# A gated recurrence and a long convolution, run among the weight blocks that follow them

## The reference, cut to what matters

```python
def hgrn2_chunked(q, k, v, log_f):
    B, S, H, DK = q.shape
    DV = v.shape[-1]
    nc = S // HG_CHUNK
    def to_chunks(t):
        return t.astype(jnp.float32).reshape(B, nc, HG_CHUNK, H, t.shape[-1]).transpose(0, 3, 1, 2, 4)
    q, k, v, log_f = to_chunks(q), to_chunks(k), to_chunks(v), to_chunks(log_f)
    b = jnp.cumsum(log_f, axis=3)
    b_last = b[:, :, :, -1:, :]
    q_t = q * jnp.exp(b)
    k_t = k * jnp.exp(-b)
    causal = jnp.tril(jnp.ones((HG_CHUNK, HG_CHUNK), dtype=bool))
    scores = jnp.einsum('bhntd,bhnsd->bhnts', q_t, k_t)
    scores = jnp.where(causal, scores, 0.0)
    o_intra = jnp.einsum('bhnts,bhnsv->bhntv', scores, v)
    k_end = k * jnp.exp(b_last - b)
    d_state = jnp.einsum('bhnsd,bhnsv->bhndv', k_end, v)
    decay = jnp.exp(b_last[:, :, :, 0, :])
    def step(state, inp):
        dec, ds = inp
        return dec[..., None] * state + ds, state
    s0 = jnp.zeros((B, H, DK, DV), jnp.float32)
    _, s_start = lax.scan(step, s0, (jnp.moveaxis(decay, 2, 0), jnp.moveaxis(d_state, 2, 0)))
    s_start = jnp.moveaxis(s_start, 0, 2)
    o_inter = jnp.einsum('bhntd,bhndv->bhntv', q_t, s_start)
    o = o_intra + o_inter
    return o.transpose(0, 2, 3, 1, 4).reshape(B, S, H, DV)
...
def hybrid_ab_mixer(x, w_in, lb, hg_norm_g, cv_w, cv_b, cv_ln_g, cv_ln_b, w_out):
    B, S, _ = x.shape
    h = x @ w_in
    q, f_pre, i_v, g, a, a_gate = jnp.split(
        h, [HG_WIDTH, 2 * HG_WIDTH, 3 * HG_WIDTH, 4 * HG_WIDTH, 4 * HG_WIDTH + CV_CH], axis=-1)
    lb = lb.astype(jnp.float32)
    f_pre = f_pre.astype(jnp.float32)
    f = lb + (1.0 - lb) * jax.nn.sigmoid(f_pre)
    k = (1.0 - lb) * jax.nn.sigmoid(-f_pre)
    log_f = jnp.log(f)
    heads = lambda t: t.reshape(B, S, HG_HEADS, -1)
    o = hgrn2_chunked(heads(q), heads(k), heads(i_v), heads(log_f))
    o = o * lax.rsqrt(jnp.mean(jnp.square(o), axis=-1, keepdims=True) + RMS_EPS)
    o = o.reshape(B, S, HG_HEADS * HG_DV) * hg_norm_g.astype(jnp.float32) * jax.nn.silu(g.astype(jnp.float32))
    u = a * jax.nn.sigmoid(a_gate)
    u = lax.conv_general_dilated(
        u, cv_w.astype(u.dtype), window_strides=(1,), padding=[(CV_K - 1, 0)],
        dimension_numbers=('NWC', 'WIO', 'NWC'), feature_group_count=CV_CH) + cv_b
    u = jax.nn.silu(layer_norm(u, cv_ln_g, cv_ln_b))
    y = jnp.concatenate([o.astype(x.dtype), u.astype(x.dtype)], axis=-1)
    return y @ w_out
...
```

## Time and profile before

| | |
|---|---|
| median of 3 runs | 1424.27 us (1422.57 to 1424.51) |
| the profiled execution | 1421.73 us, its span 1419.9 us |
| mean granted TensorE clock | 0.967 |
| TensorE busy | 1333.7 us (94% of the span) |
| VectorE busy | 857.3 us (60%) |
| ScalarE busy | 658.9 us (46%) |
| chain that ended last | PE 82%, DVE 9%, ACT 3%, DMA 3%, issue 2% |
| one weight load | 1024 KB, 5.0 to 5.3 us from issue to landing |

### The profile page before, as it was taken

One profiled execution on the slowest core, in us unless ns is written; L12 is line 12 of the kernel. 1 busy time (PEld: TensorE's weight loads), 2 busy tenths in 40 slices (PEclk: granted clock), 3 DMA queues, 4 the chain that ended last, 5 costly groups with the idle time before them and its releaser, 6 DMA issues.

```text
span 1419.9 us, 23502 instructions
## 1 busy us (share of the span) xinstructions
PE 1333.7 (94%) x9429; PEld 1248.6 (88%) x9429; DVE 857.3 (60%) x1164; ACT 658.9 (46%) x995; POOL 61.6 (4%) x72
## 2 busy tenths in 40 slices
PE   4999998999999998989997889899999999799996
PEld 4999997889998987889986788899999898799995
DVE  5566576775764544568796554655555755655555
ACT  4445676444447666345642344343433353334341
POOL 0011011000110000000000000100000000000000
PEclk9999999999989999989998899899999999899998
DMA  6555533345543332545550353655555444355552
GB/s 205 179 178 181 175 120 119 121 153 180 180 140 120 119 99 80 211 152 178 178 178 0 119 178 108 226 180 193 191 177 186 140 149 138 130 188 194 181 179 86
DMA packets 167747, 219.68 MB, mean 155 GB/s; under 512 B 3643, under 2 KB 151302, under 8 KB 167670
## 3 DMA queue, kind: packets, MB, share of 16 engines
q1 hardware_dynamic: 164422, 206.67, 44.5%
q0 software_dynamic: 3040, 11.20, 2.6%
q10 hardware_dynamic: 208, 0.74, 0.1%
HBM read 217.54 MB, written 1.05 MB: 154 GB/s over the span
## 4 chain that ended last, share of the span: by engine, by line
PE 82%; DVE 9%; ACT 3%; DMA 3%; issue 2%; POOL 0%; DVEq 0%; SPq 0%; ACTq 0%
PE bank L488 23%; PE bank L489 23%; PE bank L490 23%; DVE w_lo L1535 2%; PE bank L736 1%; DVE small L1559 1%; DVE h L1676 1%; ACT w_hi L1048 1%; DMA w_raw<-in_e_w_mem_kv 1%; PE bank L696 1%; PE bank L715 1%; PE bank L923 1%; DVE att L1597 1%; PE bank L748 1%; DMA w_raw<-in_o_w_out 1%
## 5 line engine op out<-in xcount | busy, mean ns | idle before, releaser
L1535 DVE TENSOR_TENSOR w_lo<-w_raw,w_hi 128x1024 fp32r<-128x1024 f32 x388 | 471.7, 1223 | 394.6 <-ACT w_hi L1048 391.3
L1048 ACT ACTIVATE w_hi<-w_raw 128x1024 fp32r<-128x1024 f32 x388 | 408.5, 1056 | 467.3 <-PE bank L490 368.9
L488 PE MATMUL bank<-u_hi,w_hi 128*128 128x256 f32 x1088 | 314.5, 289 | 3.3 <-DVE u_lo L1657 3.3
L489 PE MATMUL bank<-u_lo,w_hi 128*128 128x256 f32 x1088 | 311.5, 286 | 0.0
L490 PE MATMUL bank<-u_hi,w_lo 128*128 128x256 f32 x1088 | 311.3, 286 | 0.0
L488 PE MATMUL bank<-w_hi,y_hi 128*128 128x512 f32 (+1 forms) x656 | 234.6, 358 | 10.2 <-issue 7.5
L488 PE MATMUL bank<-w_hi,u_hi 128*128 128x256 f32 x832 | 238.3, 286 | 0.0
L489 PE MATMUL bank<-w_lo,u_hi 128*128 128x256 f32 x832 | 236.5, 284 | 0.0
L490 PE MATMUL bank<-w_hi,u_lo 128*128 128x256 f32 x832 | 236.5, 284 | 0.0
L489 PE MATMUL bank<-w_lo,y_hi 128*128 128x512 f32 (+1 forms) x656 | 231.1, 352 | 0.0
L490 PE MATMUL bank<-w_hi,y_lo 128*128 128x512 f32 (+1 forms) x656 | 230.6, 352 | 0.0
(11 more groups left out here) (273 smaller groups left out, 1318.6 us busy)
## 6 DMA issues: line engine op xcount, KB each, us to landing
w_raw<-in_e_w_in SPq DMA_DIRECT2D x28, 1024.0 KB, 5.0
w_raw<-in_o_w_in SPq DMA_DIRECT2D x28, 1024.0 KB, 5.2
w_raw<-in_ffn_wg SPq DMA_DIRECT2D x22, 1024.0 KB, 5.3
w_raw<-in_ffn_wu SPq DMA_DIRECT2D x22, 1024.0 KB, 5.3
w_raw<-in_ffn_wd SPq DMA_DIRECT2D x22, 1024.0 KB, 5.0
w_raw<-in_ab_w_in SPq DMA_DIRECT2D x12, 1024.0 KB, 5.2
w_raw<-in_e_w_out SPq DMA_DIRECT2D x8, 1024.0 KB, 5.0
w_raw<-in_o_w_out SPq DMA_DIRECT2D x8, 1024.0 KB, 5.2
```

Of the source, the lines that this page charges most:

```text
L488: pe.matmul(out_ap, ah, bh, start=start, stop=False, skip_group_check=True)
L489: pe.matmul(out_ap, ah, bl, start=False, stop=False, skip_group_check=True)
L1048: act.activation(w_hi[:, at:at + 1024], w_raw[:, at:at + 1024], ACT.Copy).then_inc(hi_done, 1)
L1535: v.tensor_tensor(w_lo[:, at:at + 1024], w_raw[:, at:at + 1024], w_hi[:, at:at + 1024].bitcast(F32), ALU.subtract).then_inc(lo_done, 1)
```

## The change

The mixer's small products go between the units of `ab_nat`, `xk0` and `xv0`, and between the halves of such a unit: the turn of the keys into the second `ab_nat` unit, one state product per half unit from the third on, the taps behind units, the outputs in `xk0`, the turn of y behind the first `xv0` unit, the mean between the halves of the last `xv0` unit and the variance behind it. VectorE's and ScalarE's programs are written out in the same order; `two_ahead(u, first, second)` makes the two low halves of unit u+2 with something between and behind them. The 25 taps on VectorE are split into two pairs of channels (group 0 and 1), each instruction with a wait for the previous tap of its own channel. The loads of `ab_t` alternate between input and gate, so that the first pair of channels is complete after two units. The forget gate's affine step moves from VectorE into ScalarE's logarithm (its scale and bias), the scaling of `SN` moves to ScalarE, and the small softmax that gives the bound `lb` moves to the start of the program. `ab_out` starts when the recurrence's y is there (`hg_yl`), its third unit when the convolution's is (`conv_lo`). The taps' sum moves from banks 0 and 1 to 4 and 5, mean and variance to 6 and 7, the turned y to 2 and 3.

The functions that only gather the old lines (key turn, scores, state part, scans, masks, norms) are left out here.

```diff
-            u = k8(UNIT0["ab_t"], w, 2048, 4)
+            u = UNIT0["ab_t"]
+            for j in range(2):
+                u = k8(u, w, 2048 + SEQ * j, 1)
+                u = k8(u, w, 2560 + SEQ * j, 1)
             u = k8(u, w, 512, 2)
             u = k8(u, w, 0, 2)
...
-            k8_phase("ab_nat", uh, ul, False)
-            pe.wait_ge(tL, turned("mem2"))
-            k8_phase("xk0", yh_[:, 8:16, :], yl_[:, 8:16, :], True)
-            k8_phase("xv0", yh_[:, 8:16, :], yl_[:, 8:16, :], False)
...
+            def among(phase, j, between=None):
...
+                k8_unit(u % 2, kb % 2, xh, xl, phase == "xk0", 2 * u + 1, kb - 1, between=between)
+
+            def state_and_out():
+
+                state_part(6)
+                chunk_out(0)
+
+            pe.wait_ge(tL, turned("mem2"))
+            among("ab_nat", 0)
+            among("ab_nat", 1, key_turn)
+            chunk_scores()
+            among("ab_nat", 2, lambda: state_part(0))
+            state_part(1)
+            among("ab_nat", 3, lambda: state_part(2))
+            state_part(3)
+            pe.wait_ge(up_ready, 2)
+            pe.wait_ge(hg_sm, 2)
+            conv_tap(0)
+            among("xk0", 0, lambda: state_part(4))
+            state_part(5)
+            conv_tap(1)
+            among("xk0", 1, state_and_out)
+            conv_tap(2)
+            among("xk0", 2, lambda: chunk_out(1))
+            conv_tap(3)
+            among("xk0", 3)
+            conv_tap(4)
+            among("xv0", 0)
+            conv_tap(5)
+            out_turn()
+            among("xv0", 1)
+            among("xv0", 2)
+            among("xv0", 3, conv_mean)
+            conv_var()
             pe.wait_ge(hg_yl, 1)
+            down_phase("ab_out", 0, 2)
             pe.wait_ge(conv_lo, 2)
-            down_phase("ab_out")
+            down_phase("ab_out", 2)
...
+            act.wait_ge(lb_sub, 1)
+            act.activation(lbe, lbe, ACT.Exp).then_inc(lb_exp, 1)
...
             act.wait_ge(hg_f, 1)
-            act.activation(LF, LF, ACT.Ln).then_inc(hg_ln, 1)
-            stream("xk0", 0, 2, t_dst(KT2))
+            act.wait_ge(evacuated, BANK0["ab_t"] + 6)
+            for f in range(4):
+                ins = act.activation(LF[:, f, :], SF[:, f, :], ACT.Ln, scale=oml[:, f:f + 1], bias=lb[:, f:f + 1])
+            ins.then_inc(hg_ln, 1)
+            step(UNIT0["ab_t"] + 6, copy_out(t_dst(HQ), 0), BANK0["ab_t"] + 6)
...
+            for f in range(4):
+                ins = act.activation(SN[:, f, :], SN[:, f, :], ACT.Copy, scale=oml[:, f:f + 1])
...
+            among("ab_nat", 0, copy_out(nat_dst(HV), 0))
+            among("ab_nat", 1, copy_out(nat_dst(HV), 1), keys_out)
+            diagonals(0)
+            diagonals(1)
+            among("ab_nat", 2, copy_out(nat_dst(GG), 0, ACT.Silu))
+            among("ab_nat", 3, copy_out(nat_dst(GG), 1, ACT.Silu))
+            among("xk0", 0, copy_out(t_dst(KT2), 0))
+            diagonals(2)
+            among("xk0", 1, copy_out(t_dst(KT2), 1), lambda: chunk_out(0))
+            diagonals(3)
+            among("xk0", 2, copy_out(t_dst(KT2), 2), lambda: chunk_out(1))
+            diagonals(4)
+            among("xk0", 3, copy_out(t_dst(KT2), 3))
+            diagonals(5)
+            among("xv0", 0, copy_out(nat_dst(V2), 0))
+            among("xv0", 1, copy_out(nat_dst(V2), 1), y_hi_out)
+            among("xv0", 2, copy_out(nat_dst(V2), 2))
+            among("xv0", 3, copy_out(nat_dst(V2), 3))
+            step(UNIT0["ab_out"], None, None)
...
+            def two_ahead(u, first=None, second=None):
+
+                lo_of(u + 2, 0)
+                if first is not None:
+                    first()
+                lo_of(u + 2, 1)
+                if second is not None:
+                    second()
+
...
+            def decayed():
+
+                v.wait_ge(hg_e, 2)
+                mark(v.tensor_tensor(LF, LF, SN, ALU.mult))
+                mark(v.tensor_tensor(KT, KT, SN, ALU.mult))
+                v.wait_ge(evacuated, BANK0["ab_t"] + 8)
+                mark(v.tensor_tensor(HQ, HQ, SF, ALU.mult))
+                done(hg_k)
+
...
+            tu, nu, ku, vu = (UNIT0[n] for n in ("ab_t", "ab_nat", "xk0", "xv0"))
+            mark(v.memset(UP, 0.0))
+            up(0)
+            taps(0, 2)
+            two_ahead(tu + 2, lambda: taps(0, 2))
+            taps(0, 1)
+            two_ahead(tu + 3, lambda: taps(0, 2))
+            up(1)
+            two_ahead(tu + 4, lambda: taps(1, 2))
+            taps(1, 2)
+            two_ahead(tu + 5, lambda: taps(1, 2))
+            scans()
+            two_ahead(tu + 6, lambda: taps(1, 1))
+            taps(0, 1)
+            decayed()
+            two_ahead(tu + 7)
+            taps(1, 2)
+            two_ahead(nu, lambda: taps(0, 2))
+            taps(1, 2)
+            two_ahead(nu + 1, lambda: taps(0, 1))
+            masked_scores()
+            state(0)
+            two_ahead(nu + 2, lambda: taps(0, 1), lambda: state(1))
+            state(2)
+            two_ahead(nu + 3, lambda: taps(0, 1), lambda: state(3))
+            taps(1, 1)
+            state(4)
+            two_ahead(ku, lambda: taps(1, 1), lambda: state(5))
+            gate_scale()
+            state(6)
+            two_ahead(ku + 1, lambda: taps(0, 2))
+            taps(1, 3)
+            two_ahead(ku + 2, lambda: taps(0, 2))
+            taps(1, 2)
+            out_squares()
+            two_ahead(ku + 3, out_norm)
+            taps(0, 2)
+            two_ahead(vu, lambda: taps(1, 2))
+            y_low()
+            two_ahead(vu + 1, lambda: taps(0, 3))
+            taps(1, 3)
+            two_ahead(vu + 2, lambda: taps(0, CV_K))
+            taps(1, CV_K)
+            conv_sum()
+            two_ahead(vu + 3)
             v.wait_ge(cv_mu, 1)
-            mark(v.tensor_scalar(CR, bank[4][:, 0:SEQ], 1.0 / B_W, None, ALU.mult))
+            mark(v.tensor_scalar(CR, bank[6][:, 0:SEQ], 1.0 / B_W, None, ALU.mult))
             wait_own()
             mark(v.tensor_tensor(CA, CA, CR.rearrange("p (a b) -> p a b", a=1).to_broadcast([P, 4, SEQ]), ALU.subtract))
             done(cv_c)
             v.tensor_tensor(CS, CA, CA, ALU.mult).then_inc(cv_c, 1)
-            v.wait_ge(pow_done, POW_N["hg"])
-            on3 = nat[:, 3072:4096].rearrange("p (a b) -> p a b", b=P)
-            r3 = pow_out[:, at:at + w].rearrange("p (a b) -> p a b", b=1).to_broadcast([P, 8, P])
-            mark(v.tensor_tensor(on3, on3, r3, ALU.mult))
-            wait_own()
-            mark(v.tensor_tensor(ON, ON, GG, ALU.mult))
-            done(hg_y)
+            lo_of(UNIT0["ab_out"] + 2, 0)
             v.wait_ge(cv_sd, 1)
             mark(v.reciprocal(CR, CR))
             wait_own()
             for f in range(4):
                 v.tensor_tensor(CA[:, f, :], CA[:, f, :], CR, ALU.mult).then_inc(cv_x, 1)
-            v.wait_ge(hg_yh, 2)
-            for j in range(2):
-                ins = v.tensor_tensor(yl_[:, 2 * j:2 * j + 2, :], tv(bank[6 + j][:, :]),
-                                      yh_[:, 2 * j:2 * j + 2, :].bitcast(F32), ALU.subtract)
-            ins.then_inc(hg_yl, 1)
+            lo_of(UNIT0["ab_out"] + 2, 1)
             v.wait_ge(cv_v, 4)
             mark(v.tensor_copy(yh_[:, 4:8, :], CA))
             wait_own()
             v.tensor_tensor(yl_[:, 4:8, :], CA, yh_[:, 4:8, :].bitcast(F32), ALU.subtract).then_inc(conv_lo, 1)
-            stream("ab_out", 0, 3)
+            stream("ab_out", 1, 2)
```

More of the change, by code:

```diff
@@ L928, in _ @@
[L928 to L939, removed]
@@ L968, in _ @@
                 mm.then_inc(hg_o, 1)
[L970 to L983, removed]
@@ L984, in _, with out_turn, conv_mean @@
-            mm.then_inc(hg_yt, 1)
+            def out_turn():
+                pe.wait_ge(hg_y, 1)
+                for f in range(4):
+                    for m in range(2):
+                        mm = pe.transpose(bank[2 + f // 2][:, SEQ * (f % 2) + P * m:SEQ * (f % 2) + P * m + P],
+                                          ON[:, m, P * f:P * f + P], ident)
+                mm.then_inc(hg_yt, 1)
+            def conv_mean():
+                pe.wait_ge(conv_ready, 2)
+                for f in range(4):
+                    mm = pe.matmul(bank[6][:, 0:SEQ], ones[:, :], CA[:, f, :], start=(f == 0), stop=(f == 3))
+                mm.then_inc(cv_mu, 1)
@@ new lines, in conv_var @@
+            def conv_var():
+                pe.wait_ge(cv_c, 2)
+                for f in range(4):
+                    mm = pe.matmul(bank[7][:, 0:SEQ], ones[:, :], CS[:, f, :], start=(f == 0), stop=(f == 3))
+                mm.then_inc(cv_var, 1)
+            def among(phase, j, between=None):
+                u, kb = UNIT0[phase] + j, BANK0[phase] + j
+                xh, xl = (uh, ul) if phase == "ab_nat" else (yh_[:, 8:16, :], yl_[:, 8:16, :])
+                k8_unit(u % 2, kb % 2, xh, xl, phase == "xk0", 2 * u + 1, kb - 1, between=between)
@@ L1390, in _ @@
                 .then_inc(hg_e, 1)
+            for f in range(4):
```

(33 more changed lines are left out.)

247 lines of the change are left out of this document (116 added, 131 removed).

## The result

| kernel | median of its runs, us | range | runs |
|---|---|---|---|
| before | 1423.66 | 1422.33 to 1425.04 | 10 |
| changed | 1426.93 | 1426.38 to 1429.41 | 10 |

The ratio is 1.0027, with an interval from 1.0018 to 1.0037. The change makes the kernel slower by 3.3 us (2.6 to 5.3 by the interval), where 7.7 were forecast: it lies in the stated range and in the forecast direction, but the size is under half of the forecast. The profiled execution of the changed kernel took 1426.88 us (span 1424.9), 5.15 us more than that of before.

What follows compares the result with a forecast made beforehand. TensorE, busy 94% of the span, was taken as the bound. Inline work, waits and slow clock summed to +9 us: 1430.8 against the profiled run, 1433.3 against the median; forecast 1432, range 1427 to 1438.

Steps and rivals of the forecast that it cites:

- The late tail of VectorE: Mean in the last `xv0` unit: TensorE waits 7.0 us for the convolution's sum from VectorE.
- The order at the variance: After the last `xv0` unit: centring queued behind `ab_out`'s second-unit low halves, so the variance waits 6.1 us.
- The square root behind the first `ab_out` unit: ScalarE's root follows its first `ab_out` step: 9.4 us to `conv_lo`, of which 3.9 are a wait before the third unit.
- The wait on the low halves behind `decayed`: Second `ab_nat` unit: low halves queued behind three decay products, so TensorE waits 1.8 us (0 to 3.1).
- A fall of the clock behind each of the three: Waits of 7.0 and 6.1 us each drop TensorE's clock to 0.50, the 3.9 nearly surely; 2.9 us more each.
- clock 2.9: Term added behind each of the three waits: clock low for 5.9 us, costing 2.9 us more.
- The inline pieces with their switches: Small products between weight units: 29.1 us inline on TensorE plus 1.5 for 15 changes from the stream and back.
- the start: Small softmax moved to the program's start, ahead of high and low halves TensorE awaits: 0.4 us (0 to 1.0).
- line on the hole: Hole before `ab_out`: 50.3 us become 32.8 inline and 17 of waits with nearly 9 of slow clock, +9 us.
- The tail in time: Rival: the sum is there when the mean asks, other waits stay; 0.8 us less, 1421 to 1423.5; chance 0.15.
- All covered: Rival: everything but the inline work is covered, clock holds; 18 us less, 1403 to 1406; chance 0.16.
- Lateness feeds itself: Rival: one state product in two waits 2 to 3 us for its state; 10 us more, 1442; chance 0.11.

Runs made afterwards that it cites:

- keep_warm: Changed kernel plus 12, 10 and 7 unread products on TensorE ahead of the mean, the variance and the third `ab_out` unit; 1423.78 us, ratio 1.0005.
- reordered: Changed kernel with taps forward, centring before a low half, root before ScalarE's first `ab_out` step, a low half before the decay products; 1404.99 us, ratio 0.9886.
- softmax_back: Changed kernel with the small softmax put back at its old place, with its own table load on ScalarE; 1426.20 us, ratio 1.0031.
- ylow_late: Changed kernel with VectorE's low part of the recurrence's y moved behind the convolution's sum; 1425.26 us, ratio 1.0018.
- centre_first: Changed kernel with VectorE's centring and square ahead of the second low half of the second `ab_out` unit; 1419.01 us, ratio 0.9973.
- taps_early: Changed kernel with tap instructions moved forward into VectorE's idles, the sum ahead of the last two `xv0` units' low halves; 1419.46 us, ratio 0.9982.

## Why the prediction was right in direction and off in size

**What held, step by step.** The late tail of VectorE: forecast 7.0, measured 6.69. The order at the variance: 6.1 against 5.86. The square root behind the first `ab_out` unit: 3.9 against 3.92. The wait on the low halves behind `decayed`: 1.8 against 1.54 in the row, 1.7 by the starts on both sides (671.71 to 673.41). A fall of the clock behind each of the three. The parts that the trace of before doesn't show: the logarithm in four parts 2.0 against 2.08, the scaling of `SN` 1.7 against 1.69. The experiments show for each wait that it is the named one: each disappears with its edit alone and leaves the other waits as they are.

```profile
656.68 1.28 ACT L1426 ACT_TABLE_LOAD   x1
657.98 2.08 ACT L1426 ACTIVATE nat<-nat,small 128x256 f32<-128x256 f32 x4
...
662.45 1.28 ACT L1430 ACT_TABLE_LOAD   x1
...
665.81 1.69 ACT L1435 ACTIVATE nat<-nat,small 128x256 f32<-128x256 f32 x4
```

This fence is ScalarE's timeline of the changed kernel. By the Trainium skill ("ScalarE: Activation LUTs", Table sets: the hidden batching unit) a logarithm and then an exponential need one load. The prediction went by the earlier trace rows against it, and this trace bears that out: once more there is a load ahead of the logarithm (656.68) and one ahead of the exponential (662.45), 1.28 us each, with only a copy and high halves between.

**The step that failed: the clock's 2.9 us for each wait.** Against the trace the sum ends at 818.4 and the measurement at 814.63, 3.8 less. The three terms "clock 2.9" make 8.7, and the clock cost 6.35: that is 2.35 of the 3.8. I had the length of the slow stretch from one row, the 5.9 us ahead of 790.6, and took it for a property of every fall. The other fall of the kernel before, at the variance, had lasted 5.1 us (771.81 to 776.92) and cost 2.55, and the prediction read only the length of its products. Over the twenty falls in this stretch (in the kernel before, the changed one and the variants but keep_warm and reordered) the loss goes from 1.48 to 3.11 us, with a mean of 2.40. It isn't set by the length of the wait: the one of 3.92 us cost 1.48 in the changed kernel and 3.11 in softmax_back, with the same work ahead of it. A range for each fall would have been 1.5 to 3.1.

**The other parts of the 3.8.** The last `xv0` unit starts at 760.25 and not at 761.3 (its half ends at 763.13, less half a unit). The inline pieces with their switches were 29.2 us and not 30.6 (by subtraction): a tap takes 1.54 from start to start where I had taken 1.92 and 0.1 for the change, 2.9 less for the six, and the other pieces took about 1.5 more than I had for them; the start costs 0.8 and not 0.4 (its shift is that of the turn of the mean, and holds what differs between executions), the wait 0.1 less. Together 1.1. The three waits are 0.5 shorter than forecast. That is 0.2 more than the difference of 3.8; the units and small products from the last `xv0` unit on took 0.2 longer. The prediction's line on the hole (50.3 us turned into 32.8 inline, 17 of waits and nearly 9 of clock) doesn't add up to its +9 by itself: it leaves out mean and variance, 3.8, and the 2.9 of slow clock that the kernel before had as well. The sum by moments has them.

**And the reference.** The profiled execution of before lies 1.9 us under the median of its ten runs, that of the changed kernel on its median. I had taken the middle between the sum against the one and against the other, 1432. The sum against the profiled run alone gives 1430.8, and with the true clock 1428.5. The long stretch is 4.5 us longer in the traces, the median 3.3: single executions of one kernel lie that far apart.

**The rivals.** "The tail in time" fell: the mean waited 6.69, and the idle of 5 us that spoke for it is only partly to be had (ylow_late). "All covered" gave 18 us less than before as the price of an order without these waits. In the kernel as changed it fell. The reason given against it, the second high half needed ahead of the centring, was called a dependence and was a place in a queue (centre_first); reordered then measured 17.8. That this meets the 18 so closely is in part luck: 2.25 us of wait remain that the 18 didn't have, and the inline pieces took 1.4 less than in it. "Lateness feeds itself" fell: from the key turn on no product of a state waits in the changed kernel. The gain of the change was there, then, and its queues turned it into 16.5 us of waits and 6.35 of slow clock.

## What to carry to other kernels

When small products are moved in among a weight stream, the hole they leave is won only if the vector work behind them is also moved ahead: write down each engine's queue in its new order and look for the instruction that waits for a later step while ready work stands behind it. Moving two lines past such a wait was worth 8 us here, more than the whole change had cost. Price a wait of TensorE at its own length plus the slow clock behind it, and take the second as a range over all the falls that a trace shows; a cover of useless products gives back the second part and not the first.

## What the runs showed of the hardware

The length of the slow clock behind waits of TensorE differs by a factor of two within one stretch of code (1.48 to 3.11 us lost, 3.0 to 6.2 us long from where TensorE resumes or the clock falls). The moment of the fall differs too. Behind the same wait of 3.92 us it had come 1.2 us before TensorE resumed in taps_early (0.50 from 792.84 on), and in centre_first it came 1.2 us after it, so that TensorE's first products ran at full clock there:

```profile
795.14:796.20 1.06, 1.06 (x5) 1.00 1.09 385
```

Behind idles of 2.25 us (reordered) and of 1.5 us (keep_warm) the clock stayed at 1.00; behind the idles of 3.92 us and more between the key turn and the end of `ab_out` it fell each time. The length of the idle doesn't decide it alone, though. In the kernel before an idle of 3.00 us at 737.41 left it at 1.00, and one of 2.82 us at 610.05, ahead of this stretch, did not: the eight transposes behind it took 1.97 us, where eight of the same size at 625.97 took 1.03.

```profile
610.05 1.97 PE L596 MATMUL bank<-cst,h 128*128 128x128 f32 x8 [2.82 <-DVEq L2061]
```

So the prediction's bounds of 3.0 and 4.00 us were two readings and no limit. What sets the moment and the length of a fall no run here settles; that stays open.
